# A shared stationary for both block halves of a compression MLP, and an on-chip layout in which dense operands begin at multiples of 4096 bytes

## The chip, the cores and the metric

The program runs on one core of one Trainium2 chip. The metric is the device time of the whole program in microseconds, the median of three runs of the same program. A profile is one further execution, taken with the hardware profiler.

## The reference

One decoder layer over 1024 tokens of width 1024, in float32: an RMS norm; a projection of the normed tokens (queries, three sets of keys and values, attention gates, pool inputs, merge gates); sparse attention with a compressed, a selected and a window branch; a pooling mixer; a gated merge of the two and an output projection with a residual; a second RMS norm, an MLP of 4096 hidden channels with squared ReLU, a residual, a final RMS norm. What the change touches most directly is the compression of keys and values. Each compressed token is a small MLP over a block of 32 tokens, and the blocks start 16 tokens apart:

```python
idx = jnp.arange(n_cmp)[:, None] * 16 + jnp.arange(32)[None, :]      # n_cmp = 63
blocks = kv[:, idx] + pe[None, None, :, None, :]
h = jax.nn.gelu(jnp.einsum('bclgd,ldh->bcgh', blocks, w1))           # l = 32, d = h = 64
return jnp.einsum('bcgh,he->bcge', h, w2)
```

## The kernel before

Everything runs as one hand-scheduled program. Each engine has its own list of instructions, and they meet at semaphores; all DMAs are issued from SP's queue, in the order written there.

**The dense products.** A float32 product is made from three products in the type fp32r (helper `three`, L1311 to L1315): the weights are split into `whi` and `wlo`, the moving operand into a high and a low part, and TensorE adds whi·hi, whi·lo and wlo·hi into one bank. Each of these matmuls has a stationary of 128x128 and 512 moving columns, and each loads its stationary itself. A *unit* is 128 output channels by 1024 tokens: 2 halves x 8 contraction tiles x 3 = 48 matmuls. DMA brings the weights of a unit to `wraw` (two slots), ScalarE rounds them to `whi` (L645), VectorE (in the attention part GpSimd, L620) makes `wlo` (L914).

The program goes through these parts in order:

- 15 projection units from `ahi`, `alo` (the normed tokens, transposed). Their results go to DRAM through `stage`. Between the units TensorE does small jobs (numbered steps, each in one of four banks `psX`, counted by the semaphores `misc` and `misc_ev`): after unit 6 the transposed position encodings, after unit 7 their product with the first compression matrix (`encodings_hidden`, L1390 to L1396), after unit 8 the hidden layer of the compressed keys (`hidden`, L1398 to L1405), after unit 9 that of the values, then the second layer (L1407), the pooling products (L1420, plain float32), and transposes (L1427, L1434).
- Attention, 16 steps of 128 queries and 4 heads. TensorE alternates between scores (L1482 to L1493), transposes of the probabilities (L1503), products with the values (L1514, L1515) and pieces of 16 merge-gate units, which again take `ahi`, `alo` and go to bank `psX` (`gates`, L1517 to L1527).
- 8 mixer units from `yhi`, `ylo`, `ohi`, `olo`, each led by 8 transposes (L1575), then 8 output units from `ahi`, `alo`.
- The MLP in 4 rounds: 8 units from `h2hi`, `h2lo` (up), then 8 from `ahi`, `alo` (down). The last down round is ordered by halves and ends in the final norm.

**The compression step.** `cw1` holds the first matrix with two tokens' channels (2 x 64) on the 128 partitions, and 16 such pairs per branch. A stationary is one pair: 128x64. The moving operand is every 16th column of the loaded projection (`ldA` for keys, `ldB` for values), for 2 groups x 63 blocks = 126 columns 64 bytes apart. The operands are plain float32, and each matmul stands in the profile as two instructions. The 16 matmuls of a branch accumulate in 64 rows of a bank. The bias (encodings times matrix) takes the same stationaries with one moving column. VectorE adds the bias (L1003), makes the argument of tanh (L1004 to L1006), ScalarE takes tanh (L704), VectorE finishes (L1008).

**The layout.** `place` hands out bytes of each partition one after the other, rounded up to 32. The program's first free byte is 1121, so the first tile, `wraw`, begins at 1152. `wraw`, `whi`, `wlo`, `ahi`, `alo` are multiples of 4096 bytes long, so all five begin 1152 bytes past a multiple of 4096. The small tables (`ident` to `rs`, 2464 bytes) follow. Then comes `ARENA` at byte 93728, which is 3616 past a multiple of 4096; there lie, at different times, `kS`, `kW`, then `yhi`, `ohi`, `olo`, `ylo`, then `h2hi`, `h2lo`, all at 3616 past such a multiple. `pth` and `ptl` of the attention lie at 1568, and `vS`, `vW` at 32.

## Time and profile before

| | us |
|---|---|
| median of 3 runs | 1553.82 |
| lowest and highest | 1553.58, 1554.54 |
| profiled execution | 1555.11 |
| span of the profile, first to last instruction | 1553.4 |

The mean granted clock of TensorE in the profiled execution is 0.993 of full speed. The profiled execution is 1.29 us above the median; 1.7 us of its time lie outside the span. How to read the rows further down: a matmul's duration (about 0.39 us for 512 columns) contains its way through the array and overlaps the next one, so what a matmul costs is the distance from its start to the start of the next, called its *step* here. Granted clock 1.00 is 2.4 GHz, 0.50 is 1.2 GHz.

### The profile page before, as it was taken

The page shows a single profiled execution, that of the slowest core. Times are in us where ns is not written, and L with a number is a line of the kernel's source. Part 1 is how long each engine was busy: PE and PEld are TensorE (multiplying, and loading weights), DVE is VectorE, ACT ScalarE, POOL GpSimd, SP SyncE. Part 2 cuts the span into 40 slices and gives each one's busy share as a digit, 9 for nine tenths or more (in the row PEclk, how much of TensorE's full clock was granted, in tenths as well). Part 3 has the DMA queues.
Part 4 walks back from the last instruction along what each step waited for, and adds up shares of the span by engine and source line. Part 5 has one row for each costly group of instructions (what it writes and reads, how often), then busy time and mean ns, then how long its engine had stood idle before and what let it go on. Part 6 is the DMA issues. An engine that isn't in the chain of part 4 may idle for free.

```text
span 1553.4 us, 19541 instructions
## 1 busy us (share of the span) xinstructions
PE 1519.0 (98%) x7105; PEld 1234.7 (79%) x7105; DVE 789.4 (51%) x1607; ACT 519.4 (33%) x981; POOL 82.0 (5%) x80
## 2 busy tenths in 40 slices
PE   7999999999999999899999999999999999999997
PEld 5887787888888878688887888888888888888885
DVE  5253347777777777655544353333333333333444
ACT  6111136666566665422222220123111321122232
POOL 2000000101010100000341000000000000000000
PEclk9999999999999999999999999999999999999998
DMA  6353351221221111654111111111111111111332
GB/s 192 109 172 99 105 135 41 57 57 55 58 73 58 43 63 40 209 180 132 41 54 46 49 41 54 51 44 41 54 54 41 41 53 54 41 46 49 95 109 108
DMA packets 156222, 118.23 MB, mean 76 GB/s; under 512 B 4793, under 2 KB 140517, under 8 KB 156158
## 3 DMA queue, kind: packets, MB, share of 16 engines
q1 hardware_dynamic: 156158, 117.39, 25.4%
q8 instruction: 39, 0.64, 0.2%
q14 instruction: 25, 0.20, 0.0%
HBM read 94.82 MB, written 22.54 MB: 76 GB/s over the span
## 4 chain that ended last, share of the span: by engine, by line
PE 92%; DVE 3%; ACT 2%; issue 1%; DMA 1%; DVEq 0%; ACTq 0%; SPq 0%
PE psU L1313 22%; PE psU L1314 22%; PE psU L1315 22%; PE psX L1503 4%; PE psX L1313 3%; PE psX L1315 3%; PE psX L1314 3%; PE psX L1514 2%; PE psX L1515 2%; PE psU L1482 1%; PE psU L1483 1%; PE psX L1404 1%; PE psU L1491 1%; PE psU L1490 1%; ACT prob L751 1%
## 5 line engine op out<-in xcount | busy, mean ns | idle before, releaser
L1313 PE MATMUL psU<-ahi,whi 128*128 128x512 f32 x880 | 346.3, 394 | 3.7 <-DVE alo L927 3.7
L1314 PE MATMUL psU<-alo,whi 128*128 128x512 f32 x880 | 344.4, 391 | 0.0
L1315 PE MATMUL psU<-ahi,wlo 128*128 128x512 f32 x880 | 344.1, 391 | 0.0
L645 ACT ACTIVATE whi<-wraw 128x1024 fp32r<-128x1024 f32 x104 | 109.5, 1053 | 280.7 <-PE psU L1315 279.6
L1313 PE MATMUL psU<-h2hi,whi 128*128 128x512 f32 x512 | 203.4, 397 | 0.0
L1315 PE MATMUL psU<-h2hi,wlo 128*128 128x512 f32 x512 | 203.0, 396 | 0.0
L1314 PE MATMUL psU<-h2lo,whi 128*128 128x512 f32 x512 | 203.0, 396 | 0.0
L1313 PEld LDWEIGHTS psU<-ahi,whi 128*128 128x128 f32 x880 | 166.4, 189 | 39.2 <-issue 4.9
L1315 PEld LDWEIGHTS psU<-ahi,wlo 128*128 128x128 f32 x880 | 166.3, 189 | 35.0
L1314 PEld LDWEIGHTS psU<-alo,whi 128*128 128x128 f32 x880 | 166.4, 189 | 34.5 <-issue 0.2
L1228 DVE TENSOR_TENSOR rsq<-rel 128x512 f32<-128x512 f32 x64 | 44.3, 692 | 221.1 <-ACT rel L853 221.1
L914 DVE TENSOR_TENSOR wlo<-wraw,whi 128x1024 fp32r<-128x1024 f32 x105 | 136.0, 1295 | 19.6 <-ACT whi L645 14.2
L760 ACT ACTIVATE pth<-psX 128x512 fp32r<-128x512 f32 (+1 forms) x148 | 88.1, 595 | 104.8 <-PE psX L1503 104.2
L1121 DVE TENSOR_TENSOR ptl<-psX,pth 128x512 fp32r<-128x512 f32 (+1 forms) x148 | 101.7, 687 | 41.4 <-ACT pth L760 41.0
L853 ACT ACTIVATE rel<-psU 128x512 f32<-128x512 f32 x64 | 38.3, 598 | 251.0 <-PE psU L1315 251.0
L751 ACT ACTIVATE prob<-prob,nb 128x64 f32<-128x64 f32 (+8 forms) x192 | 114.7, 599 | 19.2 <-DVE nb L1102 18.3
L1314 PEld LDWEIGHTS psU<-h2lo,whi 128*128 128x128 f32 x512 | 96.4, 188 | 23.7 <-issue 0.2
L1313 PEld LDWEIGHTS psU<-h2hi,whi 128*128 128x128 f32 x512 | 96.4, 188 | 23.7 <-issue 0.2
L1315 PEld LDWEIGHTS psU<-h2hi,wlo 128*128 128x128 f32 x512 | 96.4, 188 | 23.5
L1313 PE MATMUL psX<-ahi,whi 128*128 128x512 f32 x256 | 109.4, 427 | 1.9 <-ACT zst L774 1.9
L1240 DVE TENSOR_TENSOR f2t<-psU,r 128x512 f32<-128x512 f32 x48 | 33.2, 691 | 147.3 <-PE psU L1315 147.1
L1315 PE MATMUL psX<-ahi,wlo 128*128 128x512 f32 x256 | 101.2, 395 | 0.0
(206 smaller groups left out, 2003.5 us busy)
## 6 DMA issues: line engine op xcount, KB each, us to landing
wraw<-in_w_ff_dram SPq DMA_DIRECT2D x72, 512.0 KB, 4.0
wraw<-in_w_in_dram SPq DMA_DIRECT2D x31, 512.0 KB, 4.1
gate_scratch<-zst SPq DMA_DIRECT2D x32, 256.0 KB, 3.4
mg<-gate_scratch SPq DMA_DIRECT2D x16, 512.0 KB, 3.5
proj_scratch<-stage SPq DMA_DIRECT2D x15, 512.0 KB, 3.0
xt<-in_x_dram SPq DMA_DIRECT2D x8, 512.0 KB, 7.2
qraw<-proj_scratch SPq DMA_DIRECT2D x32, 128.0 KB, 3.0
xr<-in_x_dram SPq DMA_DIRECT2D x8, 512.0 KB, 4.4
```

The lines of the kernel that those rows point to most:

```text
L645: nc.scalar.activation(whi[:, slot], wraw[:, slot], ACT.Copy).then_inc(w_hi, 1)
L751: nc.scalar.activation(PB[it % 2][:, r, lo:hi], PB[it % 2][:, r, lo:hi], ACT.Exp, scale=2.0 ** -(g * GR + r + 1), bias=nb[:, it % 2, r, k: ...
L760: nc.scalar.activation(pth[0:rows, B % 2], psX[0:rows, B % 2], ACT.Copy).then_inc(pt_hi, 1)
L853: nc.scalar.activation(rel[:, h], psU[:, 2 * u + h], ACT.Relu).then_inc(relu[h], 1)
L914: nc.vector.tensor_tensor(wlo[:, slot], wraw[:, slot], whi[:, slot].bitcast(f32), ALU.subtract).then_inc(w_lo, 1)
L1121: nc.vector.tensor_tensor(ptl[0:rows, B % 2], psX[0:rows, B % 2], pth[0:rows, B % 2].bitcast(f32), ALU.subtract).then_inc(pt_lo, 1)
L1228: nc.vector.tensor_tensor(rsq[:, h], rel[:, h], rel[:, h], ALU.mult).then_inc(rsq_ready, 1)
L1240: nc.vector.tensor_tensor(f2t[:, h], psU[:, 2 * u + h], r2[:, cols], ALU.mult).then_inc(mul_r2, 1)
L1313: nc.tensor.matmul(ps, whi[:, slot, w], hi[:, k, cols], start=start, stop=False)
L1314: nc.tensor.matmul(ps, whi[:, slot, w], lo[:, k, cols], start=False, stop=False)
L1315: return nc.tensor.matmul(ps, wlo[:, slot, w], hi[:, k, cols], start=False, stop=stop)
L1503: last = nc.tensor.transpose(psX[0:width, B % 2, r * P:(r + 1) * P], PB[it % 2][:, r, col:col + width], ident[:])
```

## The change

Two things are done together.

**The compression.** Token l and token l + 16 of a block are the same token of two neighbouring blocks. The new stationary holds the pair of the first half in columns 0 to 63 and the pair of the second half in columns 64 to 127, so 8 matmuls of 128x128 take the place of 16 of 128x64. The moving operand now has all 64 positions (128 columns). Rows 64 to 127 of the bank are the second half's share, shifted by one block; ScalarE copies them out (`late_half_of`, `late_half_of_bias`), VectorE waits for the copy and adds both halves in the instruction that adds the bias. The matrix comes in four DMAs in place of one.

**The layout.** The small tables and `kC` are placed first and end exactly at byte 4096, `rstd` is dropped (its users write in place into `msq`), and `wraw` begins at 4096. `ARENA` is then 94208, 23 x 4096. `yraw` and `zst` change places, `gtd` moves, and SP waits for the split of `yraw` before it loads the first merge gates.

```diff
-    M_KHID, M_VHID, M_CMP, M_POOL, M_VS, M_GATE, M_VW, N_MISC = 3, 5, 6, 14, 15, 17, 18, 19
+    M_BIAS, M_KHID, M_VHID, M_CMP, M_POOL, M_VS, M_GATE, M_VW, N_MISC = 2, 3, 5, 6, 14, 15, 17, 18, 19
...
-        rstd = place("rstd", [P, TT])
...
+        kC = place("kC", [P, GROUPS, CP], f32r)
+        cursor[0] = (cursor[0] + 4095) // 4096 * 4096
+        wraw = place("wraw", [P, 2, KT, P])
+        whi = place("whi", [P, 2, KT, P], f32r)
+        wlo = place("wlo", [P, 2, KT, P], f32r)
+        ahi = place("ahi", [P, KT, S], f32r)
+        alo = place("alo", [P, KT, S], f32r)
         ARENA = cursor[0]
+        assert ARENA % 4096 == 0
...
-        zst = place("zst", [P, 2, HALF])
         yraw = place("yraw", [P, 4, S])
+        GATE_STAGE = cursor[0]
+        zst = place("zst", [P, 2, HALF])
...
-        cw1 = place("cw1", [P, 2, CBLOCK // 2, HD])
+        cw1 = place("cw1", [P, 2, CSTRIDE // 2, 2, HD])
...
-            sp.dma_start(cw1[:], cmp_w1[0].rearrange("b (j l) d h -> (l d) b j h", l=2)).then_inc(cw_in, 16)
+            for s in range(2):
+                for b in range(2):
+                    sp.dma_start(cw1[:, b, :, s], cmp_w1[0][b, s * CSTRIDE:(s + 1) * CSTRIDE].rearrange("(j l) d h -> (l d) j h", l=2)).then_inc(cw_in, 16)
...
+            sp.wait_ge(yo_lo, 2)
             load_gates(0, True)
...
+            def late_half_of_bias():
+                act.wait_ge(misc, M_BIAS)
+                nc.scalar.activation(cbh[:], psX[HD:P, (M_BIAS - 1) % 4, 0:4], ACT.Copy).then_inc(half_b, 1)
+
+            def late_half_of(b):
+                s = (M_KHID, M_VHID)[b]
+                act.wait_ge(misc, s)
+                nc.scalar.activation(cz[:], psX[HD:P, (s - 1) % 4, 0:P], ACT.Copy).then_inc(half_b, 1)
...
+                if n == 7:
+                    late_half_of_bias()
                 if n == 8:
+                    late_half_of(0)
                     gelu_tanh_of(0)
                 if n == 9:
+                    late_half_of(1)
                     gelu_tanh_of(1)
...
-                link(nc.vector.tensor_scalar(cu[:, b, 0:n2], ps[0:HD, 0:n2], cb[:, b:b + 1], None, ALU.add))
+                dve.wait_ge(half_b, b + 2)
+                link(nc.vector.scalar_tensor_tensor(out=cu[:, b, 0:n2].rearrange("p (g c) -> p g c", g=GROUPS),
+                                                    in0=ps[0:HD, 0:P].rearrange("p (g c) -> p g c", g=GROUPS)[:, :, 0:NCMP],
+                                                    scalar=cb[:, b:b + 1],
+                                                    in1=cz[:].rearrange("p (g c) -> p g c", g=GROUPS)[:, :, 1:CP],
+                                                    op0=ALU.add, op1=ALU.add))
...
-                    nc.vector.tensor_copy(cb[:], ps[0:HD, 0:2]).then_inc(misc_ev, 1)
+                    dve.wait_ge(half_b, 1)
+                    nc.vector.tensor_tensor(cb[:], ps[0:HD, 0:4:2], cbh[:, 1:4:2], ALU.add).then_inc(misc_ev, 1)
...
-                    for j in range(J):
-                        last = nc.tensor.matmul(b[0:HD, br:br + 1], cw1[:, br, j], pe2[:, br, j:j + 1], start=(j == 0), stop=(j == J - 1))
+                    for j in range(JS):
+                        last = nc.tensor.matmul(b[:, 2 * br:2 * br + 2], cw1[:, br, j].rearrange("p s h -> p (s h)"), pe2[:, br, j:J:JS],
+                                                start=(j == 0), stop=(j == JS - 1))
...
-                for j in range(J):
-                    rhs = src[:, :, 2 * j:2 * j + CSTRIDE * (NCMP - 1) + 1:CSTRIDE]
-                    last = nc.tensor.matmul(b[0:HD, 0:GROUPS * NCMP], cw1[:, br, j], rhs, start=(j == 0), stop=(j == J - 1))
+                for j in range(JS):
+                    rhs = src[:, :, 2 * j:2 * j + CSTRIDE * (CP - 1) + 1:CSTRIDE]
+                    last = nc.tensor.matmul(b[:, 0:GROUPS * CP], cw1[:, br, j].rearrange("p s h -> p (s h)"), rhs,
+                                            start=(j == 0), stop=(j == JS - 1))
```

## Rows read from the trace of the kernel before

**Rows 1.** The page, busy time, share of the span and instructions of each engine

```profile
PE 1519.0 (98%) x7105; PEld 1234.7 (79%) x7105; DVE 789.4 (51%) x1607; ACT 519.4 (33%) x981; POOL 82.0 (5%) x80
```

**Rows 2.** The page, chain that ended last, share of the span by engine

```profile
PE 92%; DVE 3%; ACT 2%; issue 1%; DMA 1%; DVEq 0%; ACTq 0%; SPq 0%
```

**Rows 3.** Timeline of TensorE around both compression steps (start, duration, what, count)

```profile
133.53 1.69 PE L1404 MATMUL psX<-ldA,cw 128*64 128x126 f32 x7
...
140.50 0.50 PE L1313 MATMUL psU<-ahi,whi 128*128 128x512 f32 x1
...
152.02 2.33 PE L1404 MATMUL psX<-ldB,cw 128*64 128x126 f32 x10
...
158.98 0.50 PE L1313 MATMUL psU<-ahi,whi 128*128 128x512 f32 x1
```

**Rows 4.** The chain in order of time: float32 products, then float32 transposes

```profile
185.07 3.44 PE psX L1420 x8
188.50 0.87 PE psX L1427 x8
```

**Rows 5.** Timeline of TensorE around the bias products, after unit 7

```profile
115.44 4.18 PE L1395 MATMUL psX<-pe,cw 128*64 128x1 f32 x64
119.55 0.79 PE L1313 MATMUL psU<-ahi,whi 128*128 128x512 f32 x1
...
125.69 0.40 PE L1315 MATMUL psU<-ahi,wlo 128*128 128x512 f32 x1
```

**Rows 6.** Windows: length, busy PE, PEld, DVE, ACT, POOL, granted clock, DMA share, GB/s

```profile
120.00:125.00 5.00, 5.00 (x13) 3.83 (x13) 4.86 (x6) 0.00 (x0) 0.00 (x0) 0.50 0.68 136
635.00:655.00 20.00, 16.48 (x78) 12.80 (x77) 14.74 (x13) 10.25 (x10) 0.00 (x0) 1.00 0.80 265
```

**Rows 7.** Timeline of TensorE at the borders of a down and an up round

```profile
916.20 0.39 PE L1313 MATMUL psU<-ahi,whi 128*128 128x512 f32 x1
...
1003.24 0.40 PE L1313 MATMUL psU<-h2hi,whi 128*128 128x512 f32 x1
...
1093.20 0.39 PE L1313 MATMUL psU<-ahi,whi 128*128 128x512 f32 x1
```

**Rows 8.** Groups by line, with counts (busy us, mean ns of one, idle before)

```profile
L1313 PE MATMUL psU<-ahi,whi 128*128 128x512 f32 x880 | 346.3, 394 | 3.7 <-DVE alo L927 3.7
L1313 PE MATMUL psU<-h2hi,whi 128*128 128x512 f32 x512 | 203.4, 397 | 0.0
L1313 PE MATMUL psX<-ahi,whi 128*128 128x512 f32 x256 | 109.4, 427 | 1.9 <-ACT zst L774 1.9
```

**Rows 9.** Timeline of TensorE, one mixer unit from its transposes to the next ones

```profile
701.12 1.03 PE L1575 MATMUL psX<-ident,xr 128*128 128x128 f32 x8
...
713.24 1.03 PE L1575 MATMUL psX<-ident,xr 128*128 128x128 f32 x8
```

**Rows 10.** Timeline of TensorE in the attention, a run of four wide matmuls

```profile
303.59 0.39 PE L1515 MATMUL psX<-ptl,vS 128*128 128x512 f32 x1
...
304.51 0.60 PE L1503 MATMUL psX<-ident,prob 128*128 128x128 f32 x4
```

**Rows 11.** Timeline of all engines after the attention (VectorE and SP's queue)

```profile
636.90 4.49 DVE L1159 TENSOR_TENSOR ylo<-yraw,yhi 128x2048 fp32r<-128x2048 f32 x2 [0.51 <-ACT yhi L806]
...
640.59 1.25 SPq L486 DMA_DIRECT2D mg<-gate_scratch  x2
...
652.05 0.68 DVE L1182 SCALAR_TENSOR_TENSOR mt<-mg,psU 128x512 f32<-128x512 f32 x1
```

**Rows 12.** Timeline near the start: SP's queue and ScalarE

```profile
12.60 0.87 SPq L359 DMA_DIRECT2D cw<-in_cmp_w_dram  x1
...
21.11 8.21 SPq L347 DMA_DIRECT2D wraw<-in_w_in_dram  x2
...
44.44 1.06 ACT L645 ACTIVATE whi<-wraw 128x1024 fp32r<-128x1024 f32 x1 [7.96 <-PE psU L1315]
```

**Rows 13.** Timeline of ScalarE: the copy out of 64 rows of a bank

```profile
626.25 0.59 ACT L767 ACTIVATE otmp<-psX 64x512 f32<-64x512 f32 x1 [1.61 <-PE psX L1515]
```

More of the change, by code:

```diff
@@ L94, in place @@
             return nc.alloc_sbuf_tensor_at(name, shape, dt, offset=off)
-        wraw = place("wraw", [P, 2, KT, P])
-        whi = place("whi", [P, 2, KT, P], f32r)
-        wlo = place("wlo", [P, 2, KT, P], f32r)
-        ahi = place("ahi", [P, KT, S], f32r)
-        alo = place("alo", [P, KT, S], f32r)
         ident = place("ident", [P, P])
@@ L115, in hybrid_trunk @@
         rs = place("rs", [P, 2, GR, 3])
+        kC = place("kC", [P, GROUPS, CP], f32r)
[5 more added lines that the diff above has]
+        alo = place("alo", [P, KT, S], f32r)
         ARENA = cursor[0]
+        assert ARENA % 4096 == 0
         kS = place("kS", [P, GROUPS, S], f32r)
         kW = place("kW", [P, GROUPS, S], f32r)
-        kC = place("kC", [P, GROUPS, CP], f32r)
         vS = place("vS", [P, TT, GROUPS, 2 * HD], f32r)
@@ L157, in hybrid_trunk @@
         otmp = place("otmp", [HD, GR * P])
+        yraw = place("yraw", [P, 4, S])
+        GATE_STAGE = cursor[0]
         zst = place("zst", [P, 2, HALF])
-        yraw = place("yraw", [P, 4, S])
         cursor[0] = REGION
@@ L186, in hybrid_trunk @@
         ldB = place("ldB", [P, GROUPS, S])
-        gtd = place("gtd", [NG, S])
         pe2 = place("pe2", [P, 2, CBLOCK // 2])
@@ L192, in hybrid_trunk @@
         cz = place("cz", [HD, P])
+        cbh = place("cbh", [HD, 4])
         kcs = place("kcs", [P, P])
+        assert cursor[0] <= GATE_STAGE - size_of([P, 4, S])
+        cursor[0] = GATE_STAGE
+        gtd = place("gtd", [NG, S])
         cursor[0] = ARENA
@@ L261, in hybrid_trunk @@
         k_hi, v_hi, gate_tanh = sem("k_hi"), sem("v_hi"), sem("gate_tanh")
-        gelu_arg, gelu_tanh = sem("gelu_arg"), sem("gelu_tanh")
+        half_b, gelu_arg, gelu_tanh = sem("half_b"), sem("gelu_arg"), sem("gelu_tanh")
         k_ready = sem("k_ready")
@@ L918, in normalize @@
                 dve.wait_ge(rms_ready, t + 1)
-                nc.vector.reciprocal(rstd[:, t:t + 1], msq[:, t:t + 1]).then_inc(rstd_ready, 1)
+                nc.vector.reciprocal(msq[:, t:t + 1], msq[:, t:t + 1]).then_inc(rstd_ready, 1)
                 dve.wait_ge(rstd_ready, t + 1)
-                nc.vector.scalar_tensor_tensor(out=xt[:, t, :], in0=xt[:, t, :], scalar=rstd[:, t:t + 1], in1=g1b[:],
+                nc.vector.scalar_tensor_tensor(out=xt[:, t, :], in0=xt[:, t, :], scalar=msq[:, t:t + 1], in1=g1b[:],
                                                op0=ALU.mult, op1=ALU.mult).then_inc(xs_ready, 1)
@@ L1282, in result @@
                 dve.wait_ge(fin_rms, t + 1)
-                nc.vector.reciprocal(rstd[:, t:t + 1], msq[:, t:t + 1]).then_inc(fin_r, 1)
+                nc.vector.reciprocal(msq[:, t:t + 1], msq[:, t:t + 1]).then_inc(fin_r, 1)
                 dve.wait_ge(fin_r, t + 1)
@@ L1286, in result @@
                     dve.wait_ge(st_out[t % 2], 16 * (t // 2))
-                nc.vector.scalar_tensor_tensor(out=ost[:, t % 2], in0=fin_bank(t), scalar=rstd[:, t:t + 1], in1=gfb[:],
+                nc.vector.scalar_tensor_tensor(out=ost[:, t % 2], in0=fin_bank(t), scalar=msq[:, t:t + 1], in1=gfb[:],
                                                op0=ALU.mult, op1=ALU.mult).then_inc(fin_o, 1)
@@ L1375, in _ @@
             J = CBLOCK // 2
+            JS = CSTRIDE // 2
             def bank():
@@ L1383, in encodings @@
             def encodings():
-                pe.wait_ge(cw_in, 64)
+                pe.wait_ge(cw_in, 16 * 7)
                 b = bank()
```

## The prediction

> **What bounds the kernel now.** I read the busy table first: TensorE is busy for 98% of the span and no other engine for more than 51% [rows 1]. Busy time of overlapping matmuls proves little, so the chain of waits comes next: 92% of it lies on TensorE [rows 2]. What shortens TensorE's own stream therefore shortens the program, and what VectorE, ScalarE or SP get in addition costs nothing as long as TensorE doesn't wait for it. Then the timeline, for the steps from one start to the next, which say more than durations. In the MLP an up and a down round have the same 8 x 48 = 384 matmuls of the same shape, back to back. The down round takes 1003.24 - 916.20 = 87.04 us, a step of 226.7 ns; the up round takes 1093.20 - 1003.24 = 89.96 us, a step of 234.3 ns [rows 7]. Weights, engines and granted clock are alike. What differs is where the moving operand lies: `ahi`, `alo` begin 1152 bytes past a multiple of 4096, as `whi` and `wlo` do; `h2hi`, `h2lo` begin 3616 past one, which is a multiple of 32 and not of 64. So a place costs 7.6 ns per matmul here.
>
> **The compression, part by part.** Each of the two hidden-layer steps holds 32 instructions: 133.53 to 140.50 and 152.02 to 158.98, 6.97 us each, 0.218 us per instruction of 126 columns [rows 3]. The change leaves 16 of 128 columns: 16 x 0.218 x 128/126 = 3.54 us, so 3.43 us less, twice: 6.9 us. Is the wider stationary dearer? Eight float32 transposes, each with a new stationary of 128x128 and 128 columns, take 0.87 us, 0.109 us each, and float32 products of 512 columns take 3.44/8 = 0.43 us [rows 4]. A float32 load of 128 columns thus fits in 0.109 us, half of the step it has to hide under. The bounds are 0 (a doubled load doubles the step) and 6.9 us; I take 6.9, since the row of the transposes is the nearer one. The same rows show that the 0.218 us are not the load but the moving columns 64 bytes apart: contiguous ones cost 0.109.
>
> The bias step takes 119.55 - 115.44 = 4.11 us for 64 instructions of one column [rows 5]; 32 of two columns take about half: 2.1 us less.
>
> Behind it stands a cost that the change doesn't name. From the end of the bias products the granted clock is at the lower of its two levels, 0.50 (1.2 GHz) [rows 6]: the 14 matmuls from 119.55 to 125.69 take 6.14 us, where 14 steps of 226.7 ns and one start after a break take 3.2 [rows 5, 7]. The fall follows 4.1 us in which the array had one column per instruction. The change leaves 2.1 us of such work. Elsewhere TensorE is idle for 3.5 of 20 us, in pieces, and the clock stays at 1.00 [rows 6]. I take it that the fall doesn't happen: 2.9 us less. The bounds are 0 and 2.9.
>
> What is added: ScalarE makes three copies out of 64 rows, of 4 or 128 columns; one with 512 columns takes 0.59 us [rows 13], an upper bound. VectorE waits for each, and behind its wait stand pooling work, the split of the next weights, and in the end TensorE, which needs the results only after the following unit: 48 steps, 10.9 us. ScalarE's wait for the bias stands in front of a weight split that has the same unit as cover. The cost is nothing; without that cover it would be three times 0.6 us. The matrix needs three more DMA issues on SP, 0.87 us each at most [rows 12]. They push the next weight load from 21.1 to about 23.7, and ScalarE takes those weights at 44.4. Bytes and run lengths stay. No cost. SP's new wait ends with the split of `ylo`, at 636.90 + 4.49 = 641.4, where the gate load was issued at 640.59; it comes 0.8 us later, the stores of `zst` behind it too, and VectorE touches the gates at 652.05 [rows 11]. No cost, with some 6 us to spare after a landing.
>
> **The layout, part by part.** After the change `ahi`, `whi`, `h2hi` and `yhi` all begin at multiples of 4096. `ahi` keeps its distance to the weights, and `h2hi` gets the same one. If the pair of places decides, `ahi` stays at 226.7 and `h2` falls to it: 3 x 512 = 1536 matmuls [rows 8] x 7.6 ns = 11.7 us. The mixer units: 713.24 - 701.12 = 12.12 us, less 0.87 for the transposes leaves 11.25 for 48, 234.4 ns [rows 4, 9]. They have the place of `h2hi`. All of the gain would be 8 x 48 x 7.7 ns = 3.0 us; I take 2.5, because behind a break the first steps are long for `ahi` too.
>
> In the attention there are 3 x 256 = 768 matmuls on `ahi` [rows 8] and some 470 wide scores and values. A run of four wide ones there takes 0.92 us, 230 ns each, though three of them have `ahi` as operand [rows 10]. The good place doesn't bring 226.7 in such short runs between transposes, so I take nothing for them. The bounds are 0 and 1240 x 3.3 ns = 4.1 us.
>
> **How a rule of the skill stands to it.** The measured steps, 226.7 and 234.3 ns, depend on the operand's place [rows 7]. The Trainium skill ("TensorE: Matmul & The Clock Gate", Part 2, step 1) says instead that moving operand and weight load have independent read ports and that a weight load takes no read bandwidth from the running matmul. By that the pair of places couldn't matter, and the layout's 14.2 us would be nothing; the trace disagrees for at least one pair of stages. The same page ("Back-to-back issue gap") gives N/2.4 + 2.5 ns, 215.7 ns for 512 columns, whatever the address; no row here is that short for this type.
>
> **The sum.** 6.9 + 2.1 + 2.9 = 11.9 us from the compression, 11.7 + 2.5 = 14.2 from the layout, 26.1 in all. Against the profiled execution, 1555.11, that gives 1529.0. The median lies 1.29 us lower, so 1553.82 - 26.1 = 1527.7. The likeliest case alone reaches from 1523.6 (the attention gains as well) to 1533.1 (the clock still falls, 2.9, and the mixers don't gain, 2.5).
>
> **Rivals.**
> The places don't matter. The up rounds are slow for another reason, such as what the other engines do meanwhile. For it: only two classes of places are in this trace. Against: all rounds show the same two steps, and the step changes with the very matmul that changes its operand [rows 7]. Then only the compression is left: 1553.82 - 11.9 = 1541.9. 13%.
> The excess goes altogether. The step falls to what float32 shows for half the rate, 0.43/2 = 215 ns [rows 4]: 11.8 ns more on 2640 + 1536 + 384 matmuls [rows 8], 53.8 us, so 1473.9. For it: at 1152 bytes even `ahi` reads run across multiples of 2048, and afterwards none does. Against: nothing in this trace shows such a step in these products. A part of it (1 ns is 4.6 us) is likelier than the whole. 10%.
> Slower. The dense stretches on `ahi` lose the state that gives 226.7, because weights and moving data now begin in the very same place of each 4096 bytes; they go at 234.3 as the up rounds do now. Place: projections, output units, down rounds, 3 x 880 = 2640 matmuls [rows 8]. Price: 2640 x 7.6 = 20.1 us against 11.9 gained and no gain on `h2`: 1562.0. It decides from 11.9/2640 = 4.5 ns on, a step of 231.2. Against: the distance of the two operands stays the same, and their places stay multiples of 128. 6%.
> The compression doesn't do what it says, because the wider load doubles the step: 1527.7 + 6.9 = 1534.6. 3%.
>
> **How the numbers follow.** The forecast has 68%. The range goes from 1519 (a ns less on all dense steps beside the forecast's low end) to 1544 (no gain from places, and 2 us lost to small things); it leaves out the full gain and the slower case. 0.2% is 3.1 us, about what a measurement of this kernel can tell from no change. All cases but the slower one lie beyond it: faster 0.92, same 0.02 for a loss that happens to balance the gain, slower 0.06.
>
> **What would show it.** Right: L1404 in 32 instructions instead of 64, the stretch between the units 3.5 us; L1395 in 32; granted clock 1.00 from 120 to 125; up and down rounds of equal length, 87.0 us; mixer units of 11.8 us; attention as long as before. Wrong: up rounds still of 90 us, down rounds of another length than 87.0, a clock of 0.50 at some new place, TensorE waiting for `half_b`'s consumers or for the gates of the first mixer unit.

## The result, and the profile after

The kernel with the change takes 1533.57 us, the median of four runs (1532.17 to 1534.08); the kernel before took 1553.94 beside it (1553.58 to 1554.54). The ratio is 0.9864, with a 95% interval from 0.9851 to 0.9877: faster by 20.4 us, where 26.1 were forecast. The time lies inside the range, 5.9 us above the point. The profiled execution took 1533.09 us, 22.0 less than that of before.

Four rows of the page answer to [rows 1, 2, 8]: busy table, chain by engine, and the costliest groups.

```profile
PE 1495.4 (98%) x7041; PEld 1230.4 (80%) x7041; DVE 790.2 (52%) x1607; ACT 520.6 (34%) x984; POOL 82.2 (5%) x80
...
PE 92%; DVE 4%; ACT 2%; DMA 1%; issue 1%; DVEq 0%; ACTq 0%; SPq 0%
...
L1340 PE MATMUL psU<-ahi,whi 128*128 128x512 f32 x880 | 346.0, 393 | 3.7 <-DVE alo L948 3.7
L1340 PE MATMUL psU<-h2hi,whi 128*128 128x512 f32 x512 | 199.6, 390 | 0.0
```

TensorE has 64 instructions fewer: 7105 - 7041 = 2 x 16 of the hidden layers and 32 of the bias. Of the groups the one on `h2hi` moved from 397 to 390 ns, the one on `ahi` by 1. VectorE's part of the chain grew from 3 to 4%. A mean duration hides more than it shows here, so again the steps, from the timeline of TensorE at the borders of a down round and of the up round behind it, against [rows 7]:

```profile
903.19 0.39 PE L1340 MATMUL psU<-ahi,whi 128*128 128x512 f32 x1
...
990.23 0.39 PE L1340 MATMUL psU<-h2hi,whi 128*128 128x512 f32 x1
...
1077.27 0.39 PE L1340 MATMUL psU<-ahi,whi 128*128 128x512 f32 x1
```

Down and up round both take 87.04 us: 226.7 ns per matmul, where the up round took 89.96. The two compression steps and the bias, same engine, same view, against [rows 3, 5]:

```profile
115.09 3.71 PE L1423 MATMUL psX<-pe,cw 128*128 128x2 f32 x32
118.66 0.78 PE L1340 MATMUL psU<-ahi,whi 128*128 128x512 f32 x1
...
131.16 3.65 PE L1433 MATMUL psX<-ldA,cw 128*128 128x128 f32 x16
...
134.46 0.59 PE L1340 MATMUL psU<-ahi,whi 128*128 128x512 f32 x1
...
146.06 3.73 PE L1433 MATMUL psX<-ldB,cw 128*128 128x128 f32 x16
...
149.44 0.59 PE L1340 MATMUL psU<-ahi,whi 128*128 128x512 f32 x1
```

The hidden layers take 3.30 and 3.38 us instead of 6.97 twice. The bias takes 118.66 - 115.09 = 3.57 instead of 4.11, although its instructions were halved. The granted clock, by windows (length, busy PE, PEld, DVE, ACT, POOL, clock, DMA share, GB/s), against [rows 6]:

```profile
115.00:118.50 3.50, 3.50 (x34) 3.46 (x32) 0.75 (x1) 0.00 (x0) 0.00 (x0) 1.00 0.49 163
118.50:121.90 3.40, 3.40 (x10) 2.72 (x11) 2.72 (x4) 1.13 (x2) 0.00 (x0) 0.50 1.06 257
...
644.20:647.50 3.30, 3.30 (x8) 2.62 (x9) 2.90 (x5) 1.03 (x2) 0.00 (x0) 0.50 0.92 281
```

Around the bias the lower level (0.50, 1.2 GHz) is still there, shorter: in both traces it begins 3.4 us into the bias (at 118.5, before at 118.9), and it now holds to 121.9, before to 125.7. And there is a second stretch of it, at the start of the second mixer unit, that the trace of before didn't have. That place once more, before in the first fence and after in the second (timeline of VectorE, TensorE and SP's queue):

```profile
650.31 1.23 DVE L914 TENSOR_TENSOR wlo<-wraw,whi 128x1024 fp32r<-128x1024 f32 x1 [2.80 <-DMA gate_scratch<-zst]
...
653.48 0.47 PE L1313 MATMUL psU<-yhi,whi 128*128 128x512 f32 x1 [1.70 <-DVE mt L1184]
```

```profile
631.42 4.73 SPq L458 DMA_DIRECT2D gate_scratch<-zst  x2
...
639.77 1.03 PE L1605 MATMUL psX<-ident,xr 128*128 128x128 f32 x8
...
641.02 1.23 DVE L935 TENSOR_TENSOR wlo<-wraw,whi 128x1024 fp32r<-128x1024 f32 x1 [4.43 <-DMA gate_scratch<-zst]
...
644.19 0.76 PE L1340 MATMUL psU<-yhi,whi 128*128 128x512 f32 x1 [3.39 <-DVE mt L1211]
...
647.66 0.40 PE L1342 MATMUL psU<-yhi,wlo 128*128 128x512 f32 x1
...
656.75 1.03 PE L1605 MATMUL psX<-ident,xr 128*128 128x128 f32 x8
```

VectorE waits for the last store of `zst`, since in the kernel before the mixers' tiles come to lie on it, and the wait was kept. Behind the wait stand the split of the mixer weights, a copy of `xT` and the gates' products `mt`; for those TensorE waits. Before, the wait ended 2.80 us after VectorE became free and TensorE lost 1.70; now 4.43 and 3.39. The chain in order of time has that store in it:

```profile
635.79 4.95 DMA gate_scratch<-zst
```

So by stages, from starts in the timelines (us, gained; a minus is lost). The stop of TensorE lies between the first and the second of the eight mixer units, so these two are taken together. The expectations further down call this stretch "the first mixer unit"; it holds two of 48 matmuls each.

| stage | forecast | measured |
|---|---|---|
| two hidden-layer steps | 6.9 | 3.67 + 3.59 = 7.3 |
| bias | 2.1 | 0.5 |
| lower clock behind the bias | 2.9 | 1.5 |
| attention, from its first probability transposes (246.62, now 237.08) to those of `xr` (637.51, now 626.45) | 0 | 1.5 |
| first two mixer units (first matmul to the third group of transposes) | part of 2.5 | 25.45 - 28.34 = -2.9 |
| the other six mixer units | part of 2.5 | 72.68 - 70.63 = 2.05 |
| four up rounds | 11.7 | 4 x 2.9 = 11.7 |
| the rest: start, end and what lies between these stages | 0 | 0.4 |

That is 22.0 us, the difference of the two profiled executions. The medians differ by 1.6 us less: the profiled execution of before lay 1.2 above its median, that of after 0.5 below.

### The profile page after: what moved, and what is told of

Same layout as the page of the kernel before. It is cut to its first block, busy times and chain, and to the rows that moved or that the text cites. A ratio compares the mean times of both kernels' runs of the same rounds, so it can differ in the third digit from the quotient of the medians.

```text
span 1531.4 us, 19420 instructions
## 1 busy us (share of the span) xinstructions
PE 1495.4 (98%) x7041; PEld 1230.4 (80%) x7041; DVE 790.2 (52%) x1607; ACT 520.6 (34%) x984; POOL 82.2 (5%) x80
## 4 chain that ended last, share of the span: by engine, by line
PE 92%; DVE 4%; ACT 2%; DMA 1%; issue 1%; DVEq 0%; ACTq 0%; SPq 0%
PE psU L1340 22%; PE psU L1341 22%; PE psU L1342 22%; PE psX L1533 4%; PE psX L1340 3%; PE psX L1342 3%; PE psX L1341 3%; PE psX L1544 2%; PE psX L1545 2%; PE psU L1512 1%; PE psU L1513 1%; PE psU L1521 1%; PE psU L1520 1%; ACT prob L772 1%; DVE ptl L1148 1%
## 5 line engine op out<-in xcount | busy, mean ns | idle before, releaser
L1340 PE MATMUL psU<-h2hi,whi 128*128 128x512 f32 x512 | 199.6, 390 | 0.0
L1342 PE MATMUL psU<-h2hi,wlo 128*128 128x512 f32 x512 | 199.2, 389 | 0.0
L1341 PE MATMUL psU<-h2lo,whi 128*128 128x512 f32 x512 | 199.2, 389 | 0.0
```

The lines of the kernel that those rows point to most:

```text
L1340: nc.tensor.matmul(ps, whi[:, slot, w], hi[:, k, cols], start=start, stop=False)
L1341: nc.tensor.matmul(ps, whi[:, slot, w], lo[:, k, cols], start=False, stop=False)
L1342: return nc.tensor.matmul(ps, wlo[:, slot, w], hi[:, k, cols], start=False, stop=stop)
```

## The experiments

My theory after the result had four parts: the distance between moving operand and weights decides the step of the dense products; the bias is bounded by its loads; a long stretch of bias work brings the lower clock; and the loss at the mixers comes from the wait for the store, not from SP's new wait. The rivals stand in the expectations. Where no number of runs is given, the kernel ran once. The kernel before ran beside them in three groups, each on another chip: 1553.93 (eight runs, 1550.67 to 1555.86) beside layout only, compression only, the arena moved by 32 bytes and SP's wait; 1554.55 (seven, 1553.68 to 1557.38) beside the wait taken away, the bias in two parts, all moved by 32 bytes, and 64 and 128 bytes; 1554.14 (nine, 1550.40 to 1554.42) beside 256 and 448 bytes, the longer program, both repairs and the four loads. A difference to the kernel after goes across groups; the ratios are each taken inside one.

### The two halves of the change

**Layout only**: the kernel after, with the compression of before (the lines shown are a part of the edit against the kernel after).

```diff
-cw1 = place("cw1", [P, 2, CSTRIDE // 2, 2, HD])
+cw1 = place("cw1", [P, 2, CBLOCK // 2, HD])
...
-                for j in range(JS):
-                    rhs = src[:, :, 2 * j:2 * j + CSTRIDE * (CP - 1) + 1:CSTRIDE]
+                for j in range(J):
+                    rhs = src[:, :, 2 * j:2 * j + CSTRIDE * (NCMP - 1) + 1:CSTRIDE]
```

> The new layout and SP's wait, with the compression as before (64 instructions per hidden layer stretch of 6.97 us, 64 bias instructions). My theory (the place of the operand sets the step): up rounds of 87.0 us instead of 90.0, so 11.7 us less, some 1.5 us less in the attention, and the first mixer unit again longer by about 2.9 us, as in the changed kernel: about 1541.5 us. Rival (the places don't matter, the changed kernel's short up rounds come from something the compression shifts in time): up rounds of 90.0 us and about 1553.9 us.

Measured: 1538.53 us (1537.65 to 1540.00, four runs), ratio 0.9903 (0.9886 to 0.9920), 15.4 us less. The up rounds take 87.04 (995.50 to the next border), the attention is 1.4 us shorter, the last six mixer units take 70.63, the first two 25.15: not longer than before, where the expectation had 2.9 more.

**Compression only**: the kernel before, with the shared stationary, its four loads and ScalarE's copies.

```diff
-            sp.dma_start(cw1[:], cmp_w1[0].rearrange("b (j l) d h -> (l d) b j h", l=2)).then_inc(cw_in, 16)
+            for s in range(2):
+                for b in range(2):
+                    sp.dma_start(cw1[:, b, :, s], cmp_w1[0][b, s * CSTRIDE:(s + 1) * CSTRIDE].rearrange("(j l) d h -> (l d) j h", l=2)).then_inc(cw_in, 16)
...
-                    last = nc.tensor.matmul(b[0:HD, 0:GROUPS * NCMP], cw1[:, br, j], rhs, start=(j == 0), stop=(j == J - 1))
+                    last = nc.tensor.matmul(b[:, 0:GROUPS * CP], cw1[:, br, j].rearrange("p s h -> p (s h)"), rhs,
+                                            start=(j == 0), stop=(j == JS - 1))
```

> The shared stationary alone, in the old layout. My theory: each hidden-layer stretch 3.4 us instead of 6.97, the bias 3.6 instead of 4.1, the lower clock behind the bias half as long (1.5 us less), up rounds unchanged at 90.0: 9.2 us less in all, about 1544.7 us. The first mixer unit takes 25.4 us as before, if its lengthening belongs to the layout. Rival (the two parts need each other): under 5 us less, or a first mixer unit of over 27 us.

Measured: 1548.36 us (1546.72 to 1550.03, five runs), ratio 0.9964 (0.9950 to 0.9979), 5.6 us less. The expectation had 9.2 less: the hidden steps are 3.7 us shorter each and the bias 0.6, as expected, but the first two mixer units take 27.69, 2.2 us more than before. Together the two halves give 21.0 us, the whole change 20.4: they add up within the spread of the runs, so the halves don't need each other, and the loss at the mixers comes with the compression, though the compression ended 490 us earlier.

### What sets the step of the dense products

Four kernels move tiles of the kernel after by a few bytes and change nothing else. In the first, what lies in the arena (`h2hi`, `kS`, `yhi` and so on) begins 32 bytes later than weights and `ahi` do.

```diff
+        cursor[0] += 32
         ARENA = cursor[0]
-        assert ARENA % 4096 == 0
```

> The changed kernel with everything from ARENA on moved up by 32 bytes; weights, ahi and alo stay at multiples of 4096. Theory A (the distance between moving operand and weights within some small power of two of bytes sets the step): up rounds back at 90.0 us, down rounds 87.0, about 1545 us. Theory B (only multiples of 4096 or crossing a multiple of 2048 matter a lot): the up rounds also 90.0, since 32 is off both; it differs from A in the other runs. Rival (32 bytes don't matter): up rounds 87.0, about 1533.5 us.

In the second everything is moved by 32 bytes, the weights too, so that all own places change and no distance does.

```diff
-        cursor[0] = (cursor[0] + 4095) // 4096 * 4096
+        cursor[0] = (cursor[0] + 4095) // 4096 * 4096 + 32
         wraw = place("wraw", [P, 2, KT, P])
```

> The changed kernel with everything from wraw on moved up by 32 bytes, so that weights and moving operands keep their distances and all begin 32 bytes past a multiple of 4096. Theory A (the distance to the weights decides): up and down rounds both 87.0 us. Theory B (each operand's own place decides): both rounds about 90, and some 27 us more than the changed kernel.

In the third `ahi` lies 64 bytes past the weights and the arena 128 (each modulo 4096), in the fourth 256 and 448.

```diff
+        cursor[0] += 64
         ahi = place("ahi", [P, KT, S], f32r)
...
+        cursor[0] += 64
         ARENA = cursor[0]
```

> Weights at multiples of 4096, ahi and alo 64 bytes past one, h2hi, h2lo, yhi, ohi and so on 128 bytes past. If only the lowest bits matter (multiples of 64 are good), both rounds stay at 87.0 us. If the good distance is a multiple of 128, down rounds, projections and output units lengthen to steps of some 234 ns and the up rounds stay at 87.0. If nothing but 4096 is good, both lengthen.

```diff
+        cursor[0] += 256
         ahi = place("ahi", [P, KT, S], f32r)
...
+        cursor[0] += 192
         ARENA = cursor[0]
```

> Weights at multiples of 4096, ahi and alo 256 bytes past one, h2hi, h2lo and the others 448 past (that is 64 below a multiple of 512). Distances of 0 have a step of 226.7 ns, 32 of 233.3, 64 of 228.9, 128 of 232.4, and the 2464 (416 past a multiple of 512) of the kernel before 234.3. Theory: the step is a function of the distance within 512 bytes, with nothing as short as 0. Then down rounds lie between 87.1 and 90.0 us, up rounds likewise. Rival (the longer the distance the more alike to none, or a distance better than 0 exists): down rounds of 87.0 or less.

Measured: 1545.42, 1532.85, 1550.43 and 1547.53 us. The borders of a down and an up round in the four traces (timeline of TensorE), in this order, each first the down round (`ahi`), then the up round (`h2hi`):

```profile
907.59 0.39 PE L1340 MATMUL psU<-ahi,whi 128*128 128x512 f32 x1
...
994.65 0.40 PE L1340 MATMUL psU<-h2hi,whi 128*128 128x512 f32 x1
...
1084.25 0.40 PE L1340 MATMUL psU<-ahi,whi 128*128 128x512 f32 x1
```

```profile
902.89 0.39 PE L1339 MATMUL psU<-ahi,whi 128*128 128x512 f32 x1
...
989.93 0.39 PE L1339 MATMUL psU<-h2hi,whi 128*128 128x512 f32 x1
...
1076.97 0.39 PE L1339 MATMUL psU<-ahi,whi 128*128 128x512 f32 x1
```

```profile
910.45 0.39 PE L1341 MATMUL psU<-ahi,whi 128*128 128x512 f32 x1
...
998.36 0.40 PE L1341 MATMUL psU<-h2hi,whi 128*128 128x512 f32 x1
...
1087.59 0.39 PE L1341 MATMUL psU<-ahi,whi 128*128 128x512 f32 x1
```

```profile
909.78 0.40 PE L1341 MATMUL psU<-ahi,whi 128*128 128x512 f32 x1
...
996.84 0.40 PE L1341 MATMUL psU<-h2hi,whi 128*128 128x512 f32 x1
...
1086.44 0.39 PE L1341 MATMUL psU<-ahi,whi 128*128 128x512 f32 x1
```

A round is 384 matmuls. The table divides by it and gives the distance of moving operand to weights in bytes, modulo 512. The reason for 512: the weight tiles of successive contraction steps are 512 bytes apart and those of the moving operand 4096, while all eight contraction steps of a round take the same time within 1.3 ns. At 64 bytes the three products differ (231.6, 226.0 and 229.1 ns for whi·hi, whi·lo and wlo·hi), and 228.9 is their mean.

| distance | from which round | us | ns per matmul |
|---|---|---|---|
| 0 | down and up, kernel after and all moved by 32 | 87.04 | 226.7 |
| 256 | down, 256 and 448 | 87.06 | 226.7 |
| 64 | down, 64 and 128 | 87.91 | 228.9 |
| 128 | up, 64 and 128 | 89.23 | 232.4 |
| 32 | up, arena moved by 32 | 89.60 | 233.3 |
| 448 | up, 256 and 448 | 89.60 | 233.3 |
| 416 (2464 bytes) | up, kernel before [rows 7] | 89.96 | 234.3 |

What follows: the own place decides nothing in these rounds, for at distance 0 they take 87.04 us with the tiles at a multiple of 4096, at 32 past one and, in the down round of before, at 1152 past one. The distance does: theory A holds and theory B falls. 0 and 256 are equally good, so the theory of the last expectation ("nothing as short as 0") is refuted and its rival's outcome came; and a distance that is a multiple of 64 doesn't suffice: 64, 128 and 448 cost 2.2, 5.7 and 6.6 ns. Of the three outcomes set out for 64 and 128 bytes the last one came, both rounds longer, but its condition, that only 4096 is good, fell with the 256 bytes. Distances other than these seven were not tried, and each kernel that moves tiles ran once; within such a run the three uninterrupted rounds of each kind repeat within 0.05 us. Why the distance matters is not shown; the runs say which distances, not what in the chip they touch.

### The mixers' first two units

**SP's new wait alone**, in the kernel before:

```diff
             load_ab(N3 + 2, N3 % 2, 2)
+            sp.wait_ge(yo_lo, 2)
             load_gates(0, True)
```

> The kernel before with nothing but SP's new wait for the split of yraw ahead of the first gate loads. If that wait, which moves the gate loads 0.8 us later and so into the way of the last store of zst, makes the first mixer unit long, it takes about 28.3 us from its first matmul to the next unit's second transposes instead of 25.4, and the time is 2 to 3 us longer. Rival (the wait is harmless, and the store took longer in the changed kernel for another reason, such as where the tiles lie): 25.4 us and no change of time.

Measured: 1554.36 us; the first two mixer units take 25.65 (25.45 without the wait) and VectorE waits 2.75 us for the store. The forecast's "no cost" holds for this wait.

**The wait for the store taken away.** In the layout after, `zst` no longer shares bytes with the tiles the mixers write first (`mt`, `ct`), so VectorE need not wait for its stores there:

```diff
-            for h in range(2):
-                dve.wait_ge(st_z[h], 16 * 2 * KT)
...
             def mix(
```

> The changed kernel without VectorE's wait for the last store of zst ahead of the mixer units; in the new layout mt and ct no longer lie on zst. My theory: this store is what the first mixer unit waits for. Without the wait VectorE goes on at about 637.5 instead of 641.0, TensorE's wait of 3.4 us for mt goes, the clock doesn't fall at 644, and the first mixer unit takes about 24 us instead of 28.3: 3.5 to 4.5 us less, about 1529.5. Rival (the gates or the weights are as late as the store): under 1 us less.

Measured: 1529.02 us (1528.28 to 1530.30, four runs), ratio 0.9832 (0.9816 to 0.9848), 4.6 us below the kernel after. VectorE and TensorE there:

```profile
639.10 1.23 DVE L935 TENSOR_TENSOR wlo<-wraw,whi 128x1024 fp32r<-128x1024 f32 x1 [1.38 <-ACT whi L653]
...
642.19 1.03 PE L1603 MATMUL psX<-ident,xr 128*128 128x128 f32 x8
...
653.96 1.03 PE L1603 MATMUL psX<-ident,xr 128*128 128x128 f32 x8
```

The split starts as soon as ScalarE has made `whi`, the gates' products are done before TensorE wants the bank, and TensorE doesn't stop at this place: 11.77 us from transposes to transposes, where the kernel after took 656.75 - 639.77 = 16.98. The first two mixer units take 24.37, 4.0 less. The wait was the cause of the stop, then. The lower clock is not gone but moved: in this trace it lies at the mixers' first matmul instead, where it costs about 1.2 us.

The length of the stop alone doesn't bring the lower clock. Compression only has a stop of 3.05 us at this place and stays at 1.00 (stop, and window over it):

```profile
646.72 0.48 PE L1335 MATMUL psU<-yhi,whi 128*128 128x512 f32 x1 [3.05 <-DVE mt L1206]
...
640.00:652.00 12.00, 8.95 (x43) 7.13 (x43) 7.82 (x11) 3.92 (x6) 0.00 (x0) 1.00 0.69 206
```

The arena moved by 32 bytes has one of 3.12 and stays at 1.00 too, while the four loads, further down, fall at one of 1.84. What brings the fall there is open.

**Why the store lands late.** With the shared stationary it takes longer from issue to landing. Two things that the compression changes were tried alone: it makes TensorE's program shorter, and it loads the matrix in four DMAs. The first experiment makes TensorE's program longer again in the kernel after, by 126 waits that are always satisfied, because a packet of 16384 bytes of the instruction queue passes during that store in the kernel after and not in the kernel before:

```diff
+                    elif 3 <= n <= 11:
+                        pe.wait_ge(consts, 1)
```

> The changed kernel with 126 waits more in TensorE's program, each for something long past, in the projections. In the kernels with the shorter TensorE program the last store of zst lands 4.7 to 5.0 us after its issue, while a packet of 16384 bytes of the instruction queue passes (at 637 to 639 us); in those with the old program it lands after 3.3 to 3.5 us, and that packet passes some 8 us before the mixers. My theory: this instruction fetch, moved by the program's length, makes the store late. Here it comes at another time, the store lands within 3.6 us, and the first mixer unit takes under 27.2 us instead of 28.3; 1 to 3 us less in all. Rival (the lateness comes from the four loads of cw1 or from something else): 28.3 us as in the changed kernel wherever the packet falls.

The second puts only the four loads into the kernel before, with TensorE's wait for them:

```diff
-            sp.dma_start(cw1[:], cmp_w1[0].rearrange("b (j l) d h -> (l d) b j h", l=2)).then_inc(cw_in, 16)
+            for s in range(2):
+                for b in range(2):
+                    sp.dma_start(cw1[:, b, 8 * s:8 * s + 8], cmp_w1[0][b, s * CSTRIDE:(s + 1) * CSTRIDE].rearrange("(j l) d h -> (l d) j h", l=2)).then_inc(cw_in, 16)
...
-                pe.wait_ge(cw_in, 64)
+                pe.wait_ge(cw_in, 16 * 7)
```

> The kernel before with cw1 loaded by four DMAs instead of one, into the old layout of the matrix, and nothing else changed. My theory: no effect; first mixer unit 25.4 us, time 1553.9. Rival for the late store (the four loads shift how later DMAs fall on the 16 engines): the last store lands after 4.7 us or more, first mixer unit of 27 us or more.

Measured: 1532.80 and 1556.14 us. VectorE's wait is 2.97 us in layout only; in the compression only, the longer program and the four loads (timeline of VectorE, one line of each):

```profile
643.56 1.23 DVE L930 TENSOR_TENSOR wlo<-wraw,whi 128x1024 fp32r<-128x1024 f32 x1 [4.16 <-DMA gate_scratch<-zst]
```

```profile
640.71 1.23 DVE L935 TENSOR_TENSOR wlo<-wraw,whi 128x1024 fp32r<-128x1024 f32 x1 [3.47 <-DMA gate_scratch<-zst]
```

```profile
649.78 1.23 DVE L916 TENSOR_TENSOR wlo<-wraw,whi 128x1024 fp32r<-128x1024 f32 x1 [2.95 <-DMA gate_scratch<-zst]
```

The four loads leave the store alone (2.95 us of wait, 3.5 from issue to landing). That kernel's first two mixer units take 27.25, 1.8 us longer and past the rival's 27, but for another reason than the rival's: at 653.8 to 657.1 the clock is at the lower level, with hardly a longer stop (TensorE waits 1.84 for `mt`). The longer program changed TensorE's instructions and didn't move the packet (637.38, before the edit 637.36), so it doesn't test the theory. The store landed after 4.0 us and the first two mixer units took 27.57, where 3.6 and under 27.2 were expected; VectorE's wait fell by 1.0 us all the same, so a spread of that size is there with nothing aimed at it.

What the DMA view says of the stretch of that store, before in the first fence and after in the second (a queue's packets, MB and share of the 16 engines; then the store, with its us from issue to landing; q8 carries the packet of 16384 bytes, q14 a smaller one):

```profile
q14 instruction: 1, 0.01, 0.5%
...
gate_scratch<-zst SPq DMA_DIRECT2D x1, 256.0 KB, 3.3
```

```profile
q8 instruction: 1, 0.02, 1.1%
...
gate_scratch<-zst SPq DMA_DIRECT2D x1, 256.0 KB, 4.9
```

In each of the fourteen traces of this study the last store was set beside that packet. It lands 3.3 to 3.5 us after its issue in the four without the shared stationary (before, layout only, SP's wait, four loads), where the q8 packet passes before the mixers, and 4.0 to 4.9 us after it in the ten with it, where it passes during the store. The packet takes 0.93 us in most of them. The two go together fourteen times of fourteen; that the one causes the other isn't shown, since no run moved the packet alone, and 0.93 us are less than the difference in four of the ten (4.7 and more). What the traces show: the late landing comes with the shared stationary, not with the layout, SP's wait or the four loads (one trace of each), and where VectorE doesn't wait for it, it costs nothing. What in the shared stationary brings it stays open.

### The bias and the clock

**The bias in two parts**, one branch ahead of unit 8 and one between its halves:

```diff
-                    encodings_hidden()
+                    encodings_hidden(0)
...
+                elif n == 8:
+                    pe.wait_ge(w_lo, n + 1)
+                    part(0, 0, KT, n % 2, ahi, alo, 2 * (n % 2), proj_before(n, n))
+                    encodings_hidden(1)
+                    part(1, 0, KT, n % 2, ahi, alo, 2 * (n % 2), proj_before(n, n))
```

> The changed kernel with the bias products in two halves, the second one between the halves of unit 8. The same instructions, but never over 1.8 us of them in a row. My theory: the granted clock stays at 1.00 there, and the stretch from unit 7 to the first hidden layer loses the time at half clock: about 1.7 us less, 1531.9. Rival (the clock falls with each stretch of narrow matmuls, or by the instant and not by what ran): two falls or one at another place, and no gain.

Measured: 1529.13 us (1528.74 to 1529.55, four runs), ratio 0.9834 (0.9817 to 0.9850), 4.4 us below the kernel after, where 1.7 were expected. Timeline and windows:

```profile
115.22 1.84 PE L1427 MATMUL psX<-pe,cw 128*128 128x2 f32 x16
116.92 0.49 PE L1340 MATMUL psU<-ahi,whi 128*128 128x512 f32 x1
...
122.51 1.84 PE L1427 MATMUL psX<-pe,cw 128*128 128x2 f32 x16
124.21 0.49 PE L1340 MATMUL psU<-ahi,whi 128*128 128x512 f32 x1
```

```profile
116.00:122.00 6.00, 6.00 (x32) 5.12 (x32) 0.17 (x1) 0.00 (x0) 0.00 (x0) 1.00 0.86 233
122.00:130.00 8.00, 8.00 (x45) 6.88 (x45) 5.20 (x7) 1.82 (x3) 0.00 (x0) 1.00 0.12 23
```

Each part takes 1.70 us, 106 ns per instruction, and the clock stays at 1.00. The unit behind the second hidden step starts at 148.07, in the kernel after at 149.44. In one piece the fall comes in all twelve traces that have it so, in two pieces of 1.7 us of the same instructions it doesn't come in either of two (this one and the next): the kind of instruction alone doesn't bring it, and the rival's two falls, or one at another place in the bias, didn't come. That gives 1.4 us against the kernel after. Another 2.2 us of this kernel's profiled execution lie in the first two mixer units (26.15), for which the edit gives no reason: the store lands after 4.2 us instead of 4.9, a difference such as the longer program showed too.

How long the lower level lasts is another matter, and the trace of the kernel after alone misleads there. Eight kernels of this study have the same shared bias in one piece. In six of them, the kernel after among them, the lower level begins 3.3 to 3.8 us after the bias does and lasts 3.4 us, and from the bias's start to the first hidden step it is 16.1 us. In the other two (the wait taken away, and 64 and 128 bytes) it begins earlier, after 2.9 and 2.2 us, and lasts 6.8, as in all four kernels with the old bias; there the same stretch takes 17.7 and 17.8, against 18.1 before. In the kernel without the wait:

```profile
117.60:124.30 6.70, 6.70 (x20) 5.54 (x20) 4.98 (x6) 1.13 (x2) 0.00 (x0) 0.50 0.73 167
```

So bias and clock together gain 2.0 us in six of these executions and 0.3 to 0.4 in two, by when the fall comes, and no edit aimed at that. In two parts the stretch takes 14.6 us in both kernels that have it, 3.5 less than before: keeping the fall away is worth 1.5 to 3.2 us here.

**Both repairs**, the bias in two parts and no wait for the store:

> The changed kernel without VectorE's wait for the last store and with the bias products in two halves. Each alone gave about 4.5 us. If they are independent (3.5 us at the mixers, 1.4 at the bias), about 1528; the 4.5 of the second alone was in part another place of the lower clock at the mixers, which the first takes away too. Rival (fully additive): 1524.5.

Measured: 1527.50 us (1525.92 to 1527.97, five runs), ratio 0.9827 (0.9814 to 0.9840): 26.6 us less than before and 6.1 less than the kernel after. Its median is the lowest of all, but its ratio's interval overlaps with those of either repair alone (0.9832 and 0.9834), so that the second repair adds to the first isn't shown by the times. Windows of its trace over the bias and the mixers' start:

```profile
105.00:127.00 22.00, 22.00 (x114) 18.72 (x113) 9.81 (x13) 2.98 (x5) 0.00 (x0) 1.00 0.71 188
628.00:632.00 4.00, 4.00 (x13) 3.18 (x12) 3.57 (x2) 0.56 (x2) 0.00 (x0) 0.61 0.97 318
```

TensorE is busy without a gap in the first, at 1.00. A stretch at the lower level is left where the mixers begin. The repairs together give less than the sum of their single gains (4.6 + 4.4 = 9.0), which fits the 2.2 us of the second that lay at the mixers, where the first removes the stop; the expectation's 1528 came, the rival's 1524.5 didn't.

## Why the prediction was right, and where it was not

**Two hidden-layer steps, 6.9: right.** 7.3. The load of 128 columns does hide under a step of 0.21 us.

**The bias, 2.1: mis-sized, 0.5.** "32 of two columns take about half" is the step that failed. With one or two moving columns nothing hides the load, and the load grows with the columns of the stationary. Groups of loads, kernel before and kernel after (the count of the first is of its stretch at full clock):

```profile
L1395 PEld LDWEIGHTS psX<-pe,cw 128*64 128x64 f32 x58 | 3.5, 138 | 0.4 <-issue 0.4
```

```profile
L1423 PEld LDWEIGHTS psX<-pe,cw 128*128 128x128 f32 x32 | 3.8, 194 | 0.1
```

The step from one to the next went from (118.80 - 115.44)/58 = 58 ns to 3.57/32 = 112 ns (109 where the clock is at 1.00). That the moving columns went from one to two isn't the reason: the transposes, with 128 of them, step at 109 as well. The row for it was in my hands: eight transposes with a 128-column float32 stationary step at 0.109 us [rows 4]. I used it as the cover the hidden step needs and not as the floor for the bias; 32 x 0.109 = 3.5 us was the forecast to make. The Trainium skill ("TensorE: Matmul & The Clock Gate", "LDWEIGHTS (loading the stationary operand)") says that a load takes its columns divided by 1.2, in ns, whatever the rows: 107 for 128 columns and 53 for 64. The trace agrees within 6 ns, 112 and 58.

**The clock behind the bias, 2.9: half of it, 1.5, in this trace.** "I take it that the fall doesn't happen" rested on a bias of 2.1 us. It lasted 3.6, and the fall came. "From the end of the bias products" was misread too: the lower level begins 3.4 us into them, at 118.9 of 119.55. The two parts of 1.7 us, with which it stays at 1.00, bear out the link of the fall to this stretch. That it lasted only half as long isn't a fixed gain of the change: of eight executions with this bias two have the 6.8 us of before. The 1.5 us are in part luck.

**What is added, 0: right for SP's wait and the copies, wrong for the store.** "No cost, with some 6 us to spare after a landing" looked at the gates' load. It did not look at what else VectorE waits for there. The wait for the last `zst` store already cost TensorE 1.70 us before; it had no slack, so each microsecond of a later landing reaches TensorE: 4.43 - 2.80 = 1.6 us at VectorE, 3.39 - 1.70 = 1.7 at TensorE. Behind the stop the clock fell: from 644.19 eight matmuls take 3.5 us, where eight steps of 0.23 take 1.8. These 1.7 us and the 1.7 of the stop, less what the layout gives back in these two units, are the 2.9. That the longer stop brought the fall isn't shown: stops of 3.05 and 3.12 us pass without one, one of 1.84 doesn't. I named "a clock of 0.50 at some new place" and "TensorE waiting for the gates of the first mixer unit" as what would show the forecast wrong, and gave them no price; the wait came in this place, for the store and not for the gates.

**The layout, 11.7 + 2.5: right for the up rounds, 11.7.** The last six mixer units gave 2.05. In layout only, where nothing else disturbs, the mixers as a whole gave 2.35, near to the 2.5. That the pair of places decides is confirmed, and more closely than claimed: by the kernel with all tiles moved. The rival that places don't matter is refuted by the same runs, and so is what the prediction took from the rule of independent read ports (the Trainium skill, "TensorE: Matmul & The Clock Gate", Part 2, step 1), that the pair of places couldn't matter; whether the ports are what the distance touches, no run shows. The rival that the whole excess goes is refuted by 226.7 ns as the best of all distances tried, and the slower one by down rounds that stay at 87.04.

**Attention, 0 (bounds 0 to 4.1): 1.5.** It comes with the layout: 1.4 in layout only, none in compression only, and none with the arena moved by 32 bytes, where the stretch takes 390.9 us as before (389.4 in the kernel after). It shows no single wait; I didn't split it by product.

The sum: short by 1.6 at the bias, 1.4 at the clock, 3.3 at the mixers, 26.1 - 6.3 = 19.8; more by 0.4 at the hidden steps, 1.5 in the attention and 0.4 in the rest gives 22.1, against 22.0 between the profiled executions and 20.4 between the medians.

## What to carry to other kernels

When instructions are merged, ask of each what bounds it: a merge halves the time of those bound by moving columns, and gives almost nothing to those bound by the load of a stationary that gets twice as wide. When a product of high and low parts streams one operand against freshly loaded weights, look at the byte distance of the two tiles and not at their alignment; here a good distance was worth 3% of a stage at no cost (87.04 against 89.96 us). Before the length of a stretch at the lower clock is put down to an edit, look at more than one execution. And before calling a moved DMA free, look for every wait that has no slack now, however far behind the edit; where a layout makes a wait needless, take it out.

## What the runs showed of the hardware that was not expected

- The step of these matmuls depends on the distance of the moving operand to the weights: 226.7 ns at 0 and 256 bytes modulo 512, 228.9 at 64, 232.4 at 128, 233.3 at 32 and 448, 234.3 at 416.
- A float32 stationary of 128 columns under two moving columns steps at 109 ns with the clock at 1.00 (106 in runs of 16), one of 64 columns under one at 58.
- The granted clock fell to 0.50 between 2.2 and 3.8 us after the start of such work where it stood in one piece (twelve traces), and stayed at 1.00 where it stood in pieces of 1.7 us (two). With the same bias it stayed low for 3.4 us in six executions and for 6.8 in two.
- At the stop of the mixers it fell at one of 1.84 us (four loads only) and not at ones of 1.70 (the kernel before), 3.05 (compression only) and 3.12 us (arena moved by 32 bytes).
- The last store of `zst`, 256 KB, lands between 3.3 and 4.9 us after its issue, with the same DMAs issued around it.
